# Sum units in the output projections of the LRU and of the attention: two per pass, with low parts written in place

## The reference

```python
h = h + (gelu(gate_br) * rec) @ w_out + b_out            # RG-LRU block, w_out 2048 x 2048
h = h + swiglu(rmsnorm(h), ffn_w_in[0], ffn_w_out[0])    # FFN, width 5632
k_sh, v_sh = shared_kv(h)
h = h + causal_attention(q, k_sh, v_sh) @ w_o            # MLA block, w_o 2048 x 2048
h = h + swiglu(rmsnorm(h), ffn_w_in[1], ffn_w_out[1])
```

## Time and profile before

| | us |
|---|---|
| median of three runs | 1967.44 |
| the profiled execution: time, span | 1967.33, 1965.5 |
| PE busy | 1957.2 |
| DVE busy | 1713.6 |
| ACT busy | 1163.6 |
| POOL busy | 153.4 |
| LRU's projection, units 0 to 15 | about 215.2 to 302.5 |
| attention's projection, units 0 to 15 | about 1169.9 to 1267.8 |

### The profile page before, as it was taken

One profiled execution on the slowest core, in us unless ns is written; L12 is line 12 of the kernel. 1 busy time (PEld: TensorE's weight loads), 2 busy tenths in 40 slices (PEclk: granted clock), 3 DMA queues, 4 the chain that ended last, 5 costly groups with the idle time before them and its releaser, 6 DMA issues.

```text
span 1965.5 us, 23834 instructions
## 1 busy us (share of the span) xinstructions
PE 1957.2 (100%) x9348; PEld 1646.3 (84%) x9348; DVE 1713.6 (87%) x1931; ACT 1163.6 (59%) x1465; POOL 153.4 (8%) x143
## 2 busy tenths in 40 slices
PE   9999999999999999999999999999999999999999
PEld 8898888888888888888898888888888888888887
DVE  7979846899999999999976886479999999999997
ACT  5488545656565556666666664555565565566563
POOL 1000210010001101000002110000001100010000
PEclk9999999999999999999999999999999999999999
DMA  8664663566666666666564335456666666666664
GB/s 283 207 200 161 225 215 129 194 204 200 196 208 198 206 199 196 209 195 203 182 223 147 114 127 194 143 178 208 198 206 201 197 201 202 204 202 200 204 198 148
DMA packets 160685, 378.62 MB, mean 193 GB/s; under 512 B 6298, under 2 KB 11172, under 8 KB 160452
## 3 DMA queue, kind: packets, MB, share of 16 engines
q1 hardware_dynamic: 160276, 376.06, 57.9%
q0 software_dynamic: 272, 1.13, 0.2%
q10 hardware_dynamic: 32, 0.01, 0.0%
HBM read 375.08 MB, written 2.10 MB: 192 GB/s over the span
## 4 chain that ended last, share of the span: by engine, by line
PE 92%; issue 5%; DVE 1%; POOL 1%; ACT 0%; DMA 0%; POOLq 0%; SPq 0%; ACTq 0%
PE bank L1935 78%; PE bank L2133 6%; PE bank L2131 3%; PE bank L1896 2%; PE bank L1928 1%; PE bank L2117 1%; PE bank L1919 1%; DVE w_lo L1120 0%; POOL stats L1877 0%; PE bank L2130 0%; DMA raw<-in_lru_w_in 0%; ACT w_hi L654 0%; POOL stats L1875 0%; PE bank L2097 0%; POOL stats L1873 0%
## 5 line engine op out<-in xcount | busy, mean ns | idle before, releaser
L1935 PE MATMUL bank<-w_hi,act 128*128 128x512 f32 x3440 | 1104.3, 390 | 0.0
L1935 PEld LDWEIGHTS bank<-w_hi,act 128*128 128x128 f32 x3440 | 645.7, 188 | 133.5
L1935 PE MATMUL bank<-raw_lo,act 128*128 128x512 f32 x1464 | 569.9, 389 | 0.0
L654 ACT ACTIVATE w_hi<-raw 128x2048 fp32r<-128x2048 f32 (+1 forms) x240 | 448.5, 1882 | 155.6 <-PE bank L1935 66.4
L1935 PEld LDWEIGHTS bank<-raw_lo,act 128*128 128x128 f32 x1464 | 274.9, 188 | 56.5
L1120 DVE TENSOR_TENSOR raw_lo<-raw,w_hi 128x2048 fp32r<-128x2048 f32 x116 | 264.0, 2286 | 21.3 <-ACT w_hi L654 21.1
L731 ACT ACTIVATE w_lo<-t_raw 128x1024 fp32r<-128x1024 f32 x108 | 114.2, 1058 | 272.8 <-DVE t_raw L1177 272.8
L1190 DVE TENSOR_TENSOR raw_lo<-raw,w_hi 128x2048 fp32r<-128x2048 f32 x108 | 246.6, 2283 | 0.0
L1120 DVE TENSOR_TENSOR w_lo<-raw,w_hi 128x2048 fp32r<-128x2048 f32 (+1 forms) x84 | 183.1, 2190 | 64.2 <-ACT w_hi L654 63.9
L1935 PE MATMUL bank<-w_lo,act 128*128 128x512 f32 x580 | 190.8, 389 | 0.0
L2133 PE MATMUL bank<-act,w_hi 128*128 128x512 f32 x480 | 169.0, 396 | 0.0
(11 more groups left out here) (247 smaller groups left out, 2365.7 us busy)
## 6 DMA issues: line engine op xcount, KB each, us to landing
raw<-in_ffn_w_in SPq DMA_DIRECT2D x176, 1024.0 KB, 5.4
raw<-in_ffn_w_out SPq DMA_DIRECT2D x88, 1024.0 KB, 5.3
raw<-in_lru_w_in SPq DMA_DIRECT2D x28, 1024.0 KB, 5.5
raw<-in_lru_w_out SPq DMA_DIRECT2D x16, 1024.0 KB, 4.9
raw<-in_w_o SPq DMA_DIRECT2D x16, 1024.0 KB, 5.5
raw<-in_w_ukv SPq DMA_DIRECT2D x8, 1024.0 KB, 5.4
raw<-in_w_uq SPq DMA_DIRECT2D x8, 768.0 KB, 4.6
raw<-in_w_dkv SPq DMA_DIRECT2D x8, 576.0 KB, 4.3
```

The source lines that it names most:

```text
L654: A.activation(flat_chunk(w_hi, SLOT[c], size), flat_chunk(raw, SLOT[c], size), ACT.Copy).then_inc(w_hi_done, 1)
L1935: i = T.matmul(bank[:, :], x_part, w_part, start=first and n == 0, stop=last and n == 2)
```

## The change

Four of the 16 units of each projection become sum units: units 4 and 6 in pass one, 10 and 11 in pass two (`PROJ_SUMS`). The LRU's projection makes four sides, the attention's three: its unit 10 uses the side that unit 6 made. The low parts of all chunks of both projections are now written in place, so their slots are free only when TensorE has used the chunk. The LRU's projection keeps 4 slots, the attention's now has 5. In each pass ACT copies one shared bank (`p1_out`), and DVE adds up the shared banks and adds them to `h` (`shared_to_h`), at steps 6 and 11. TensorE waits for that before unit 8, which starts in banks that pass one shared, and before the transposes in units 13 and 14. Unit 10 waits until the results of pass one are in `h`. The rest of the diff renumbers counters.

The tables, and SP's condition for a load:

```diff
+PROJ_SUMS = (4, 6, 10, 11)
+PROJ_PLACE = {4: 0, 6: 1, 10: 0, 11: 1}
+PROJ_SET = {0: {4: 0, 6: 1, 10: 2, 11: 3}, 2: {4: 0, 6: 1, 10: 1, 11: 2}}
+PROJ_MADE = {0: (4, 6, 10, 11), 2: (4, 6, 11)}
+PROJ_LAST = (6, 11)
...
-def in_ffn(c):
-
-    return C_UP0 <= c < C_DKV or c >= C_UP1
+def in_place(c):
+
+    return C_LOUT <= c < C_DKV or c >= C_WO
...
-                    sp_.wait_ge(chunk_used if in_ffn(before) else w_lo_done, before + 1)
+                    sp_.wait_ge(chunk_used if in_place(before) else w_lo_done, before + 1)
```

DVE's program of a projection:

```diff
                     if n == KT // 2 - 1:
                         results_to_h(d, 0, KT // 2)
-                    split(DOWN_C[d] + n + 4)
+                    if n in PROJ_LAST:
+                        half = n // PROJ_UNITS
+                        if half:
+                            dve.wait_ge(h_sq, NB * d + 2)
+                        shared_to_h(d, half, SUM_BLOCKS * (d // 2) + half, SHARED * (d // 2) + half)
+                    if n + 4 in PROJ_SUMS:
+                        proj_sums(d, n + 4)
+                    proj_split(d, n + 4)
...
+            def proj_sums(d, n):
+
+                if n in PROJ_MADE[d]:
+                    kt = 2 * proj_rows(d, n)
+                    source_ready(dve, d, kt // 4)
+                    dve.wait_ge(chunk_used, DOWN_C[d])
+                    make_side(proj_side_no(d, n), kt, PROJ_SET[d][n])
+                sums(DOWN_C[d] + n, proj_unit_no(d, n), PROJ_PLACE[n], DOWN_TILES)
```

ACT's:

```diff
-                    split(DOWN_C[d] + n + 4)
+                    if n in PROJ_LAST:
+                        p1_out(d, n, n // PROJ_UNITS)
+                    after = n + 4
+                    if after in PROJ_SUMS:
+                        side_no = proj_side_no(d, after) if after in PROJ_MADE[d] else None
+                        split_sums(DOWN_C[d] + after, proj_unit_no(d, after), PROJ_PLACE[after], DOWN_TILES, side_no,
+                                   PROJ_SET[d][after])
+                    else:
+                        split(DOWN_C[d] + after)
```

TensorE's unit:

```diff
+                if n == PROJ_UNITS:
+                    pe.wait_ge(u_done, SHARED * (d // 2) + 1)
                 pe.wait_ge(w_lo_done, DOWN_C[d] + n + 1)
-                if v == KT // 2 - 1:
+                if n in PROJ_SUMS:
+                    first = n in (PROJ_SUMS[0], PROJ_SUMS[2])
+                    if n in PROJ_MADE[d]:
+                        pe.wait_ge(g_sum_lo, proj_side_no(d, n) + 1)
+                    if first and half:
+                        pe.wait_ge(h_done, NB * d + 2)
...
+                    i = sum_unit(c, PROJ_PLACE[n], PROJ_SET[d][n], k0, result, shared_banks(d, half), first,
+                                 n in PROJ_LAST, None, DOWN_TILES)
```

More of the change, by code:

```diff
@@ L634, in pass_banks, with shared_banks @@
             return banks if d % 2 else [banks[n] for n in (0, 2, 1, 3)]
+        def shared_banks(d, half):
+            return banks_of((half + d) % 2 == 1)[1]
         def sum_tiles(t, e):
@@ L715, in gT_out, with split_sums @@
                 e.then_inc(gT_act, 1)
[L717 removed]
+            def split_sums(c, q, e, tiles=UP_TILES, side_no=None, j=None):
                 b21, b12 = tiles[1], tiles[2]
@@ L722, in split_sums @@
                 slot_free(act, c)
[L723 to L726, removed]
+                if side_no is not None:
+                    act.wait_ge(g_sum, side_no + 1)
+                    A.activation(side_parts(j)[0], side_raw(j), ACT.Copy).then_inc(g_sum_hi, 1)
                 loaded(act, c)
@@ L741, in down_split, with p1_out @@
                     g_no = down_sum_no(n)
-                    split_sums(c, down_unit_no(f, n), g_no % 2, DOWN_TILES, 2 * len(DOWN_SUMS) * f + g_no)
+                    split_sums(c, down_unit_no(f, n), g_no % 2, DOWN_TILES, SIDE0[2 * f + 1] + g_no, g_no % 3)
                 else:
                     split(c)
+            def p1_out(d, n, half):
+                act.wait_ge(chunk_used, DOWN_C[d] + n + 1)
+                if d + half:
+                    act.wait_ge(h_shared, 2 * d + half)
+                A.activation(gtmp[:, 0, :], shared_banks(d, half)[0][:, :], ACT.Copy).then_inc(p1_done, 1)
             def two_pass(f):
@@ L760, in two_pass @@
                     if v == DOWN_SUMS[-1]:
-                        p1_out(n, half)
+                        p1_out(d, n, half)
                     if n % 2:
@@ L1207, in shared_add, with make_side @@
                 dve.wait_ge(u_done, n_done + 1)
+            def make_side(o, kt, j):
+                a11, a21 = feat[:, kt, 0:P], feat[:, kt, P:SEQ]
+                a12, a22 = feat[:, kt + 1, 0:P], feat[:, kt + 1, P:SEQ]
+                to = side_raw(j)
+                V.tensor_tensor(to[:, 0, :], a22, a21, ALU.subtract).then_inc(g_sum_step, 1)
+                V.tensor_tensor(to[:, 2, :], a11, a21, ALU.subtract)
+                dve.wait_ge(g_sum_step, 2 * o + 1)
+                V.scalar_tensor_tensor(out=to[:, 1, :], in0=to[:, 0, :], scalar=-1.0, in1=a11,
+                                       op0=ALU.mult, op1=ALU.subtract).then_inc(g_sum_step, 1)
+                dve.wait_ge(g_sum_step, 2 * o + 2)
+                V.tensor_tensor(to[:, 3, :], a12, to[:, 1, :], ALU.add).then_inc(g_sum, 1)
@@ L1226, in down_split, with proj_split @@
+            def proj_split(d, n):
+                if n not in PROJ_SUMS:
+                    return split(DOWN_C[d] + n)
+                if n in PROJ_MADE[d]:
+                    side_low(proj_side_no(d, n), PROJ_SET[d][n])
+                split_sums(DOWN_C[d] + n, proj_unit_no(d, n), PROJ_PLACE[n])
             def down_split(f, n):
@@ L1243, in results_to_h @@
                 result = pass_banks(d, half)
[L1244 to L1247, removed]
+                dve.wait_ge(h_shared, 2 * d + half + 1)
                 for b in (0, 1):
@@ L1276, in into_next, with shared_to_h @@
                     split(c_next + n)
+            def shared_to_h(d, half, n_p1, n_done):
+                if d == half == 0:
+                    dve.wait_ge(bout_added, 1)
+                shared_add(shared_banks(d, half), n_p1, n_done)
+                for t in range(NT):
+                    hb = h[:, t, (2 * half) * W:(2 * half + 1) * W]
+                    V.tensor_tensor(hb, hb, gtmp[:, t, :], ALU.add)
+                for t in range(NT):
+                    hb = h[:, t, (2 * half + 1) * W:(2 * half + 2) * W]
+                    i = V.tensor_tensor(hb, hb, mix[:, t, :], ALU.subtract)
+                i.then_inc(h_shared, 1)
             def project(d):
@@ L1289, in two_pass @@
                 d = 2 * f + 1
[L1291 to L1302, removed]
                 for n in range(DOWN_UNITS - 4):
@@ L1973, in sum_unit @@
                 product(shared[3], s3, t3, first, last)
-                if first:
+                if first and gT_needed:
                     pe.wait_ge(gT_act, gT_needed)
@@ L2057, in two_pass @@
                     if v == 0:
-                        pe.wait_ge(u_done, (FB + 2) * f + FB + half)
+                        pe.wait_ge(u_done, SHARED * f + FB + 2 + half)
                     if n % 2 == 0:
```

76 lines of the change are left out of this document (44 added, 32 removed).

## The result

| | before | after |
|---|---|---|
| median, us | 1967.83 (6 runs, 1967.33 to 1968.74) | 1984.64 (6 runs, 1982.10 to 1986.25) |
| profiled execution: time, span | 1967.33, 1965.5 | 1983.3, 1981.5 |
| DVE busy, us | 1713.6 | 1780.1 |

The change makes the kernel slower: ratio 1.0084, interval 1.0073 to 1.0095. The forecast was 1980.1 with a range of 1973 to 1987, and slower with a chance of 0.87. The median lies inside that range, but 1.6 us above the forecast's own one, 1977 to 1983.

The account below looks back on a forecast made before the run. PE was taken to bound the kernel (92% of the chain), with DVE's added work not fitting in time; LRU +10.6 and attention +2.1 us, gain deducted, took 1967.4 to 1980.1, own range 1977 to 1983, wide range 1973 to 1987.

Parts of the forecast that it names:

- The gain: Both projections: eight sum units with 3 matmuls less each save 5.4 us, 2.7 in each projection, all on the path.
- LRU, unit 4: LRU's projection, unit 4: POOL's bias adds take turns with DVE and hold it, so PE stalls 5.9 us.
- Rival B: LRU's unit 4: POOL doesn't hold DVE; LRU +4.3 and attention +2.1 us, time 1973.8; chance 0.12.
- What moves the loads: LRU's projection: in-place loads land 4.9 us later, within the lead of 16.3 us; nothing late in the attention's.
- LRU, the rest: LRU's projection after unit 4: DVE is the bound; stalls of 1.3, 0.8, 2.0 and 3.3 us at units 6, 8, 10, 11.
- Rival C: Stall at LRU's unit 4: TensorE falls to its lower clock, 0 to +3.6 us, about +2, time 1982; chance 0.15.
- Attention: Attention's projection: stalls of 0.9, 1.1 and 2.8 us at units 4, 6 and 11; less 2.7 gained, +2.1 us.
- The sum: Both projections: 10.6 us for the LRU's and 2.1 for the attention's make +12.7 us, time 1980.1.
- Rival A: Steps 0 to 7 of both projections: the lead of four units hides it all; -5.4 us, time 1962.0; chance 0.08.

Follow-up runs that it names:

- experiment 6: The changed kernel with sum units only at unit 11 of the LRU's projection and units 6 and 10 of the attention's: 1965.53 us, ratio 0.9989.
- experiment 1: The changed kernel with POOL's two bias adds cut to one column each, the rest of the bias left out: 1976.58 us, ratio 1.0042.
- experiment 2: The changed kernel with POOL's bias added in eight instructions of 512 columns in place of two of 2048: 1983.80 us, ratio 1.0079.
- experiment 3: The changed kernel without sum units in either projection, only the low parts in place: 1968.15 us, ratio 1.0000.
- experiment 7: The changed kernel with sum units 4 and 6 of the LRU's projection alone, plain units elsewhere: 1978.30 us, ratio 1.0052.
- experiment 5: The kernel before, with one added wait of TensorE ahead of the LRU's unit 4 until POOL has added the bias: 1974.80 us, ratio 1.0036.
- experiment 4: The changed kernel with sum units in the attention's projection alone, plain units in the LRU's: 1972.16 us, ratio 1.0020.
- experiment 8: The changed kernel with sum units 10 and 11 of the LRU's projection alone, plain units elsewhere: 1969.04 us, ratio 1.0007.

## Why the prediction was right, and where it was off

- **The gain**, 5.4 us on the path: right. In experiment 6 the units that don't stop PE give their 0.68 each.
- **LRU, unit 4**, 5.9 us because POOL takes turns with DVE: 5.77, and experiments 1 and 2 show the mechanism. Rival B, by which POOL doesn't hold DVE, had 1973.8; with POOL's adds cut away the kernel takes 1976.6. The difference of 2.8 is a stretch of half clock (1.7 us) and the 0.3 us that each of six stops costs beside its length, less 0.75 because the stops are that much shorter than B's.
- **What moves the loads**: late by one load, inside the lead. Right alone (experiment 3). With sum units the load of chunk 9 sets unit 8's wait, as the forecast has it. No run has sum units with the low parts in a place of their own, so what the loads cost beside sum units isn't measured.
- **LRU, the rest**: stalls of 1.3, 0.8, 2.0 and 3.3 at units 6, 8, 10 and 11 were forecast; 0, 1.73, 1.95 and 1.40 were measured. By the rows, unit 6's vanished because matmuls at half clock gave DVE 2.25 us ahead of it (DVE is done with unit 6's operands at 254.2, and chunk 9's load, which starts with the end of unit 5, at about 255.4). Most of it came out at unit 8: a stall at unit 6 would have hidden 1.3 us of that load. Without a wait at unit 6, unit 8's is 1.7 in the sum of rival B, and 1.73, 1.83 and 1.77 in the changed kernel and in experiments 1 and 7; where unit 6 waits for 6.34, in experiment 2, it is 0.35. Unit 11's shrank for the second stretch of half clock; without it unit 11 waits 3.03 (experiment 1), near the 3.3.
- **Rival C**, the lower clock, came true beside the forecast. By "TensorE: Matmul & The Clock Gate", Part 1, of the Trainium skill an idle array goes back to 1.2 GHz; the windows at 0.50 and experiment 5 agree. I had given it 0 to +3.6, about +2. In the changed kernel 3.95 us went at half clock, 3.2 came back as shorter waits at units 6 and 11, and 0.9 of that went again at unit 8: 1.65 net, near the +2. That it came out so near is in part luck, since I had looked at one stretch, behind unit 4; there are two in this execution's LRU projection, and only one or none there in experiments 7 and 1.
- **Attention**, 0.9, 1.1 and 2.8: measured 0.62, 0.98 and 2.70. Right.
- **The sum**, 12.7 us, against 16.0 in the profiled execution. By terms: half clock +3.95; unit 6 -1.3; unit 11 -1.9; unit 8 +0.9; units 4 and 10 -0.2; the attention's three stops -0.5; some 0.3 us for each of seven stops, +2.3. That makes 12.7 + 3.3 = 16.0. Two terms were put at nothing in the sum: the clock, which I kept as a rival in place of a term (1.65 net), and the 0.3 a stop (2.3), because I took a stop to cost its idle time. The forecast's own range, 1977 to 1983, left no room for the two; the wider one held because its upper end was drawn for the clock and for longer stalls. The median lies another 1.3 above the profiled execution, as in the runs of experiment 4: the runs above 1985 have a clock of 0.996, the profiled one 0.997.
- **Rival A**, all hidden by the lead of four units, was the assumption to refuse: it holds for the three passes with one sum unit that experiment 6 has, and for no pass with two. The LRU's pass one, where POOL's bias is, was not run with one.

## What to carry to other kernels

When work moves from the engine that bounds to one that is 62% busy (54.3 of 87.4 us), count it step by step in program order, over the lead that the buffers give, and not over the stage, and count in what shares the engine's turns (here POOL). A saving of three matmuls (0.68 us) that costs 6 us elsewhere is worth placing only where the helper has that time in hand: three units without a stop gain 2 us, eight with stops lose 17. And where TensorE is stopped for several us, add the half clock behind it, about 2 to 3 us here, to the stop.

## What the runs showed of the hardware

- A stop of 4.56 us cost 7.1 us by the medians and 8.0 in the profiled execution (experiment 5). All four stops of that length or more in the projections (4.56; 5.77 in the changed kernel; 5.80 and 6.34 in experiments 7 and 2) were followed by 4.3 to 6.2 us of work at half clock.
- Behind shorter stops the clock fell in some executions and not in others. It was at half for some 3.4 us behind one of 1.95 that came 13 us after one of 1.73 (the changed kernel), of 3.01 (experiment 2) and of 2.66 (experiments 1 and 2), and stayed at 1.00 behind those of 1.83, 1.94 and 3.03 (experiment 1), 1.77 and 1.58 (experiments 7 and 8) and 2.70 (the changed kernel and experiment 4). Behind those of under 1 us in the projections it stayed at 1.00. What decides in between isn't shown.
- A stop costs 0.24 to 0.32 us more than the idle time that the profile gives it, since idle time is counted from the end of a matmul's 0.39 us and the pace is 0.227.
- A DVE instruction of 0.28 us took 1.38 beside POOL's pieces. Short instructions pay the most in turns: they wait out the other's whole instruction each time.
